# Which of two token blocks is chosen first: four heads of the scattered block move into the query stage, the gathered block moves to the gate stage

## The chip, the cores and the metric

The kernel runs on one core of one Trainium2 chip. The metric is the device time in microseconds, from the start of the program to its end, as the median of three runs. Below, PE is TensorE, DVE is VectorE, ACT is ScalarE, POOL is GpSimd and SP is SyncE, which here issues most of the transfers.

## What is computed

512 tokens of width 1024 pass through a mixer (two gated recurrences, a short convolution, an output projection), a layer norm, and then a layer of single-neuron experts with product keys. The change touches only the expert layer:

```python
def peer(x, w_q, k1, k2, u_tab, v_tab):          # 8 heads, 128 keys a side, 16 experts a head
    q = (xt @ w_q).reshape(t, PEER_HEADS, 2, PEER_HALF)
    s1 = jnp.einsum("thd,kd->thk", q[:, :, 0], k1)
    s2 = jnp.einsum("thd,kd->thk", q[:, :, 1], k2)
    v1, i1 = lax.top_k(s1, PEER_TOPK)
    v2, i2 = lax.top_k(s2, PEER_TOPK)
    cand_s = v1[..., :, None] + v2[..., None, :]
    top_s, pos = lax.top_k(cand_s, PEER_TOPK)
    idx = take(i1 * N_KEYS + i2, pos)
    g = jax.nn.softmax(top_s, axis=-1)
    ...
    act = jax.nn.gelu(jnp.einsum("cd,ced->ce", xb, u_tab[ib]))
    return jnp.einsum("ce,ced->cd", gb * act, v_tab[ib])
```

Each token takes 16 of 16,384 experts for each of 8 heads, 128 in all.

## The kernel before

The tokens are four blocks of 128, and the blocks go three ways. **Blocks 0 and 1** get a dense matrix of gates, made on PE from one-hot vectors of the chosen keys. **Block 2** (`ST`) gets its rows of the same gate matrix in DRAM, by scattering: each of its 128 slots (8 heads by 16) is one indirect transfer that adds 128 single numbers to the matrix, `GateCells.scatter`, L247. **Block 3** (`DT`, "far") doesn't use the dense product: for each of its 128 slots an indirect transfer gathers one expert row of 8 KB for each token (`GatherPath.start`, L1117, ring of three tiles), DVE takes the dot product (`dot`, L1136), ACT the gelu and the gate (`weigh`), and DVE adds the weighted second half of the row to a sum (`add`, L1157). `far.use(i)` is the i-th of these 256 operations of DVE: dot 0, dot 1, add 0, dot 2, add 1, and so on. For blocks 0 to 2 PE multiplies all 128 blocks of expert rows with the tokens (`ActPipeline.product`, L952, 24 matmuls for each), and later the gated activations with all second halves (L1746).

**Stages.** All five engines run programs written out by hand, one loop pass for each block m of expert rows. Products 0 to 15 lie in the *query stage* (query step n does 24 matmuls of the query projection, L1383, then product n, then 8 score matmuls, L1371), 16 to 18 follow it, and products 19 to 95 are the steps s = 0 to 76 of the *gate stage*, m = 19 + s. The *expert stage* has 128 steps; in the first 64 every second one also does a product, 96 to 127.

Product m needs the low parts of its weights, `ut_lo`. Until product 26 POOL makes them (`acts.lower`, L979); in step s = 7 (`BY_POOL`) DVE takes over (L986) and POOL keeps only the indirect transfers. Each engine works strictly in the order of its program, so what stands behind a waiting instruction waits too. POOL in query step n does `acts.lower(n - 1)`, then the low part of the query weights `wq_lower(n)` (L1320), then what else it has.

**Choosing.** After the top-16 searches, `Selection` turns positions into keys and gates for one block: places, match, weigh, add up for each side, then softmax. "Early" picks handle four heads after query step 7 (`PICK_AT`), and end in query step 9 with a list of addresses, on which the first indirect transfer waits. "Late" picks handle the rest in the gate stage, at the steps of `SELECT_AT` (eight parts for each block). `far_ops(m)` says how many of the 256 far operations DVE does beside block m; the gathers are started by what these sums allow. `scattered_by` spreads the 128 scatters over the gate stage; the first scatter of each head waits until all 16 of the head before it have landed. The one-hot groups (96, PE L1609, 8 matmuls for each pair of groups) run from s = 10 to 63.

## Time and profile before

| | us |
|---|---|
| Median of 3 runs (lowest, highest) | 1611.48 (1607.8, 1616.52) |
| The profiled execution's own time | 1613.08 |
| Its span from first to last instruction | 1611.1 |
| PE busy | 1519.5 |
| DVE busy | 1223.0 |
| ACT busy | 768.3 |
| POOL busy | 634.4 |

The span is 2 us shorter than the execution's time, which also holds the start and the end around it. Busy time is an average over stages with different limits, so it says where the work is and not what ends the kernel: the query stage lies at about 299 to 470 us, the gate stage at 483 to 929 us, the expert stage after that.

### The profile page before, as it was taken

To read this page: it belongs to the slowest core of one execution; us is meant where nothing else is said; L and a number is where in the kernel's file an instruction comes from. 1 tells how busy PE (TensorE), PEld (TensorE's weight loads), DVE (VectorE), ACT (ScalarE), POOL (GpSimd) and SP (SyncE) were. 2 spreads that over 40 slices of the span, in tenths; PEclk is the share of its full clock that TensorE was granted. 3 is DMA by queue.
4 is the path that set the end of the run, shared out by engine and by line. 5 is a ranking of instruction groups with operands and counts; after the bars stand their busy time and mean duration, and the time that the engine had idled before them with its cause. 6 is when DMAs were issued, how large, how long until landed. Compare 5 with 4: busy or idle time off the path is not lost.

```text
span 1611.1 us, 21027 instructions
## 1 busy us (share of the span) xinstructions
PE 1519.5 (94%) x7484; PEld 1329.3 (83%) x7484; DVE 1223.0 (76%) x2135; ACT 768.3 (48%) x1427; POOL 634.4 (39%) x400
## 2 busy tenths in 40 slices
PE   7999999999987899899988889999999999999996
PEld 5877657799987889898988878888888888888785
DVE  7569985678997768686664388888888877888775
ACT  3559970323224467676754244444444444444432
POOL 4843352664545777787778111111111111111100
PEclk9999999999999999999999899999999999999998
DMA  7438310433445678899999999999999989999972
GB/s 271 170 93 239 92 43 0 154 125 109 179 139 171 185 233 228 215 268 274 271 265 269 349 343 354 344 333 354 346 346 338 350 319 348 345 358 354 337 254 93
DMA packets 214791, 397.00 MB, mean 246 GB/s; under 512 B 97312, under 2 KB 155040, under 8 KB 198304
## 3 DMA queue, kind: packets, MB, share of 16 engines
q1 hardware_dynamic: 176384, 259.17, 48.6%
q0 software_dynamic: 36864, 134.30, 25.5%
q10 hardware_dynamic: 1440, 2.19, 0.4%
q8 instruction: 60, 0.98, 0.2%
q14 instruction: 43, 0.35, 0.1%
HBM read 349.40 MB, written 46.20 MB: 246 GB/s over the span
## 4 chain that ended last, share of the span: by engine, by line
PE 54%; POOL 17%; DVE 14%; DMA 6%; issue 6%; ACT 2%; SPq 0%; DVEq 0%; POOLq 0%; ACTq 0%
PE bank L1746 29%; POOL gate_matrix L247 13%; PE bank L952 13%; PE bank L787 5%; DMA gate_matrix<-gate_values,gate_cells 3%; PE bank L1383 2%; POOL gathered L1117 2%; PE bank L842 2%; DMA gate_rows_then_feed<-activations 2%; DVE xc L684 1%; DMA gathered<-in_peer_rows,expert_rows 1%; PE bank L828 1%; POOL rms L487 1%; PE bank L799 1%; DVE hit_late L1035 1%
## 5 line engine op out<-in xcount | busy, mean ns | idle before, releaser
L952 PE MATMUL bank<-xhi,ut_hi 128*128 128x384 f32 x1024 | 356.1, 348 | 30.4 <-DVE ut_lo L986 15.7
L1117 POOL DMA_INDIRECT gathered<-in_peer_rows,expert_rows x128 | 140.4, 1097 | 584.0 <-DVE gather_sum L1157 553.5
L952 PE MATMUL bank<-xhi,ut_lo 128*128 128x384 f32 x1024 | 349.3, 341 | 0.0
L952 PE MATMUL bank<-xlo,ut_hi 128*128 128x384 f32 x1024 | 349.0, 341 | 0.0
L247 POOL DMA_INDIRECT gate_matrix<-gate_values,gate_cells x128 | 244.6, 1911 | 63.9 <-issue 36.7
L1746 PE MATMUL bank<-v_hi,w_hi 128*128 128x512 f32 x760 | 236.3, 392 | 8.3 <-DVE w_lo L1851 8.3
L1786 ACT ACTIVATE v_hi<-gate_rows_then_feed 128x1024 fp32r<-128x1024 f32 x128 | 135.7, 1061 | 221.0 <-PE bank L1746 221.0
L1746 PE MATMUL bank<-v_lo,w_hi 128*128 128x512 f32 x760 | 235.3, 391 | 0.0
L1746 PE MATMUL bank<-v_hi,w_lo 128*128 128x512 f32 x760 | 235.2, 391 | 0.0
L952 PEld LDWEIGHTS bank<-xhi,ut_hi 128*128 128x128 f32 x1024 | 198.0, 193 | 36.1 <-DVE ut_lo L986 17.3
L1136 DVE SCALAR_TENSOR_TENSOR gathered<-gathered,h 128x1024 f32<-128x1024 f32 x128 | 156.1, 1220 | 70.9 <-DMA gathered<-in_peer_rows,expert_rows 70.8
L952 PEld LDWEIGHTS bank<-xlo,ut_hi 128*128 128x128 f32 x1024 | 197.7, 193 | 1.8
L952 PEld LDWEIGHTS bank<-xhi,ut_lo 128*128 128x128 f32 x1024 | 197.0, 192 | 0.0
L986 DVE TENSOR_TENSOR ut_lo<-u_raw,ut_hi 128x1024 fp32r<-128x1024 f32 x101 | 123.8, 1225 | 80.6 <-ACT ut_hi L962 74.2
L1834 DVE TENSOR_TENSOR v_lo<-gate_rows_then_feed,v_hi 128x1024 fp32r<-128x1024 f32 x128 | 156.4, 1222 | 33.4 <-ACT v_hi L1786 32.7
L967 ACT ACTIVATE gel<-bank 128x384 f32<-128x384 f32 x128 | 62.5, 488 | 243.9 <-PE bank L952 237.0
L1746 PEld LDWEIGHTS bank<-v_hi,w_hi 128*128 128x128 f32 x760 | 142.5, 189 | 37.7 <-DVE v_lo L1834 7.2
L1746 PEld LDWEIGHTS bank<-v_lo,w_hi 128*128 128x128 f32 x760 | 143.4, 189 | 30.6
L1746 PEld LDWEIGHTS bank<-v_hi,w_lo 128*128 128x128 f32 x760 | 143.2, 188 | 30.3
L1157 DVE SCALAR_TENSOR_TENSOR gather_sum<-gathered,expert_gelus,gather_sum 128x1024 f32<-128x1024 f32 x127 | 166.3, 1309 | 0.2
L962 ACT ACTIVATE ut_hi<-u_raw 128x1024 fp32r<-128x1024 f32 x128 | 135.0, 1055 | 16.7 <-DMA u_raw<-in_peer_u_turned 16.6
L979 POOL TENSOR_TENSOR ut_lo<-u_raw,ut_hi 128x1024 fp32r<-128x1024 f32 x27 | 66.2, 2454 | 86.7 <-ACT ut_hi L962 86.4
(246 smaller groups left out, 2406.5 us busy)
## 6 DMA issues: line engine op xcount, KB each, us to landing
u_raw<-in_peer_u_turned SPq DMA_DIRECT2D x128, 512.0 KB
gate_rows_then_feed<-in_peer_rows SPq DMA_DIRECT2D x128, 512.0 KB
gate_rows_then_feed<-gate_matrix SPq DMA_DIRECT2D x128, 192.0 KB
activations<-gel SPq DMA_DIRECT2D x96, 192.0 KB
gate_rows_then_feed<-activations SPq DMA_DIRECT2D x96, 192.0 KB
u_raw<-in_w_in_chunks SPq DMA_DIRECT2D x28, 512.0 KB, 4.1
gate_matrix<-gate_zeros SPq DMA_DIRECT2D x8, 1024.0 KB, 7.4
wq<-in_peer_wq_chunks SPq DMA_DIRECT2D x16, 512.0 KB, 3.9
```

Of the source, the lines that this page charges most:

```text
L247: self.nc.gpsimd.indirect_dma_start(out=self.flat, out_offset=bass.IndirectOffsetOnAxis(ap=self.at[:, k:k + 1], axis=0), in_=self.gate[:, ...
L787: ins = mm(z_bank(n)[:, :], w[n % 2][:, k, :], x[:, k, :], start=(i == 0), stop=(i == 3 * KD - 1))
L952: ins = self.nc.tensor.matmul(self.bank[b + r % 2][:, 0:DTOK], u[r % 2][:, k, :], x[:, k, 0:DTOK], start=(i == 0), stop=(i == 3 * KD - 1))
L962: self.nc.scalar.activation(self.hi[r % 2][:, :, :], self.by_channel(r), ACT.Copy).then_inc(self.hi_ready, 1)
L979: self.nc.gpsimd.tensor_tensor(out=self.lo[r % 2][:, :, :], in0=self.by_channel(r), in1=self.hi[r % 2][:, :, :].bitcast(F32), op=ALU.subtr ...
L986: self.nc.vector.tensor_tensor(out=self.lo[r % 2][:, :, :], in0=self.by_channel(r), in1=self.hi[r % 2][:, :, :].bitcast(F32), op=ALU.subtr ...
L1117: self.nc.gpsimd.indirect_dma_start(out=self.tile[q % RING][:, :], out_offset=None, in_=self.table, in_offset=bass.IndirectOffsetOnAxis(ap ...
L1136: self.nc.vector.scalar_tensor_tensor(out=half, in0=half, scalar=1.0, in1=self.x, op0=ALU.mult, op1=ALU.mult, accum_out=self.act[:, q:q + ...
L1157: ins = V.scalar_tensor_tensor(out=self.sum[:, :], in0=half, scalar=weight, in1=self.sum[:, :], op0=ALU.mult, op1=ALU.add)
L1746: ins = mm(bank[2 + 2 * tb + half][:, :], w[r][:, tb * P:(tb + 1) * P], v[r][:, half * HALF_D:(half + 1) * HALF_D], start=begins, stop=ends)
L1786: S.activation(v_hi[r][:, :], v_raw[r][:, :], ACT.Copy).then_inc(v_hi_ready, 1)
L1834: V.tensor_tensor(out=v_lo[r][:, :], in0=v_raw[r][:, :], in1=v_hi[r][:, :].bitcast(F32), op=ALU.subtract).then_inc(v_lo_ready, 1)
```

## The change

The four heads chosen in the query stage are now heads 0 to 3 of block 2, the scattered one, not of block 3. Their gates and their addresses (`list_cells`, one DVE instruction more than `list_rows`) go to `GateCells`, whose tiles are allocated earlier for it. POOL scatters two slots in each query step from n = 10 on, one with each of the blocks 16 to 25, and two with each block from 26 on; `SCATTERED_BY` replaces `scattered_by`. 22 of the 128 scatters so come before step s = 7, where none did, and the last one lies in s = 59, where it was s = 66. The wait of the gathers on their first list, and the asserted distance of three query steps between list and first gather, are gone from the query stage; a second list of block 2 (heads 4 to 7) comes in gate step 1, and a scatter of slot 64 waits for it.

Block 3 is now chosen whole, eight heads, in gate steps 2 to 5, and its first three gathers start in s = 6. The far operations of the query stage (10) are gone. In the gate stage there are one in every second step from s = 8, one in every step from s = 15, none in 28 to 35, and three in two steps after s = 65: 64 in all before the expert stage, where it was 75. In the expert stage DVE does two in each of the first 64 steps, as before, and after them seven in six steps, where it was one in each, so that block 3 is done at step 119 and not 117. Blocks 0 and 1 are chosen in steps 7 to 14 and 28 to 35 (before 4 to 8 and 20 to 27), and the one-hot groups run from s = 16 to 64, in 49 steps for 54.

```diff
@@ -64,25 +64,31 @@
 GROUPS = P // NT
 HALF_GROUPS = GROUPS // 2
 BY_POOL = 7
-SELECT_AT = {ST: (0, 0, 1, 1, 2, 2, 3, 3), 0: (4, 4, 5, 5, 6, 6, 7, 8), 1: tuple(range(20, 28)),
-             DT: tuple(range(32, 40))}
-TURN_AT = {9: 0, 29: 1}
-HOT_AT, HOT_STEPS = 10, 54
-SCATTER_AT, SCATTER_STEPS = 7, 60
+SELECT_AT = {ST: (0, 0, 0, 0, 1, 1, 1, 1), DT: (2, 2, 3, 3, 4, 4, 5, 5), 0: tuple(range(7, 15)),
+             1: tuple(range(28, 36))}
+TURN_AT = {15: 0, 36: 1}
+HOT_AT, HOT_STEPS = 16, 49
+FIRST_GATHER = 6
 
 
 def far_ops(m):
 
     s = m - BY_QUERIES
-    if m < QC - 3:
+    if s < FIRST_GATHER + 2 or 28 <= s < 36:
         return 0
-    if s < 0:
-        return 2 if m < QC else 4 if m == QC else 0
-    if s < HOT_AT or 20 <= s < 28:
+    if s < 15:
+        return 1 - s % 2
+    return 2 - s % 2 if s > 65 else 1
+
+
+def scatters(m):
+
+    if m < 10:
         return 0
-    return 2 if s in (11, 13, 15, 17, 19, 29) else 1
-
-
+    return 2 if m < QC else 1 if m < BY_QUERIES + BY_POOL else 2
+
+
+SCATTERED_BY = [min(SLOTS, sum(scatters(e) for e in range(m))) for m in range(MADE + 1)]
 FAR_BY = [sum(far_ops(e) for e in range(m)) for m in range(MADE + 1)]
 FAR_FROM = FAR_BY[MADE]
 
...
@@ -236,12 +242,25 @@
                       self.zeros[:, :].unsqueeze(1).broadcast_to([P, self.ROWS, P])).then_inc(self.zeroed, 16)
 
 
+    def list_cells(self, eng, link, sel, q, n):
+
+        V, at, size = self.nc.vector, slice(q * TOPK, (q + n) * TOPK), n * TOPK
+        link(V.scalar_tensor_tensor(out=self.row[:, at], in0=sel[:, 0, 0:size], scalar=float(KEYS),
+                                    in1=sel[:, 1, 0:size], op0=ALU.mult, op1=ALU.add))
+        if q == 0:
+            eng.wait_ge(self.token_ready, 1)
+        link(V.tensor_scalar(out=self.at[:, at], in0=self.row[:, at], scalar1=float(DTOK),
+                             scalar2=self.token[:, 0:1], op0=ALU.mult, op1=ALU.add))
+        V.sem_inc(self.listed, 1)
+
+
     def scatter(self, eng, k):
 
         q = k // TOPK
         if k == 0:
             eng.wait_ge(self.zeroed, 16 * self.ZEROED)
-            eng.wait_ge(self.listed, 1)
+        if k in (0, EARLY_HEADS * TOPK):
+            eng.wait_ge(self.listed, 1 + k // (EARLY_HEADS * TOPK))
         if k % TOPK == 0 and q > 0:
             eng.wait_ge(self.landed[(q - 1) % 2], 16 * TOPK * ((q - 1) // 2 + 1))
         self.nc.gpsimd.indirect_dma_start(
...
@@ -1337,13 +1346,13 @@
                 blk = h[:, n - 1, :]
                 link(G.tensor_tensor(out=blk, in0=blk, in1=ln[:, 0, :], op=ALU.mult))
                 link(G.tensor_tensor(out=blk, in0=blk, in1=ln[:, 1, :], op=ALU.add))
-            for q in range(started_by(n - 1), started_by(n)):
-                far.start(eng, q)
+            for k in range(SCATTERED_BY[n], SCATTERED_BY[n + 1]):
+                cells.scatter(eng, k)
         for m in range(QC - 1, BY_QUERIES + 1):
             acts.lower(eng, m, m)
-            if m == QC:
-                for q in range(started_by(QC - 1), started_by(QC)):
-                    far.start(eng, q)
+            if QC <= m < BY_QUERIES:
+                for k in range(SCATTERED_BY[m], SCATTERED_BY[m + 1]):
+                    cells.scatter(eng, k)
 
     def tensor(eng):
         mm, tr = nc.tensor.matmul, nc.tensor.transpose
@@ -1435,17 +1442,15 @@
                 link(top16(lambda tb: cand[:, tb, :], lambda tb: crep[:, tb, :],
                            lambda tb: top[:, tb, q, :], lambda tb: pos[:, tb, q, :]))
             if n == PICK_AT:
-                picks.places(link, DT, 0, EARLY_HEADS)
+                picks.places(link, ST, 0, EARLY_HEADS)
                 picks.match(link, 0, EARLY_HEADS)
                 picks.choose(link, 0, EARLY_HEADS)
             elif n == PICK_AT + 1:
                 picks.match(link, 1, EARLY_HEADS)
                 picks.choose(link, 1, EARLY_HEADS)
             elif n == PICK_AT + 2:
-                link(picks.softmax(eng, link, 1, EARLY_HEADS, far.gate[:, 0:EARLY_HEADS * TOPK]))
-                picks.list_rows(link, far, 0, EARLY_HEADS)
-        for e in range(FAR_BY[QC], FAR_BY[QC + 1]):
-            far.use(eng, e)
+                link(picks.softmax(eng, link, 1, EARLY_HEADS, cells.gate[:, 0:EARLY_HEADS * TOPK]))
+                cells.list_cells(eng, link, picks.sel, 0, EARLY_HEADS)
 
     def released(eng):
 
...
@@ -1495,7 +1500,7 @@
         hot_ready, hot_scaled, g_done, g_copied = (sem(n) for n in ("one_hot_ready", "one_hot_scaled", "g_done", "g_copied"))
         g_stored = [[sem(f"g_{part}_stored{i}") for part in ("low", "high")] for i in range(2)]
         nth = {tb: i for i, tb in enumerate(SELECT_AT)}
-        heads_of = lambda tb: (EARLY_HEADS, QH - EARLY_HEADS) if tb == DT else (0, QH)
+        heads_of = lambda tb: (EARLY_HEADS, QH - EARLY_HEADS) if tb == ST else (0, QH)
 
         def vector(eng):
             link = Chain(eng, chain)
@@ -1513,21 +1518,16 @@
                     picks.weigh(link, part // 4, n)
                 elif part in (3, 6):
                     if part == 3:
-                        after(eng, selT_done, {ST: 0, 0: 0, 1: 1, DT: 2}[tb])
+                        after(eng, selT_done, int(tb == 1))
                     picks.add_up(link, part // 4, n)
                 elif tb == DT:
-                    link(picks.softmax(eng, link, nth[DT] + 1, n, far.gate[:, q * TOPK:(q + n) * TOPK]))
-                    picks.list_rows(link, far, q, n)
-                elif tb < ST:
+                    link(picks.softmax(eng, link, nth[DT] + 1, n, far.gate[:, :]))
+                    picks.list_rows(link, far)
+                elif tb == ST:
+                    link(picks.softmax(eng, link, nth[tb] + 1, n, cells.gate[:, q * TOPK:(q + n) * TOPK]))
+                    cells.list_cells(eng, link, sel, q, n)
+                else:
                     picks.softmax(eng, link, nth[tb] + 1, QH, sel[:, 2, :]).then_inc(sel_ready, 1)
-                else:
-                    link(picks.softmax(eng, link, nth[tb] + 1, QH, cells.gate[:, :]))
-                    link(V.scalar_tensor_tensor(out=cells.row[:, :], in0=sel[:, 0, :], scalar=float(KEYS),
-                                                in1=sel[:, 1, :], op0=ALU.mult, op1=ALU.add))
-                    eng.wait_ge(cells.token_ready, 1)
-                    link(V.tensor_scalar(out=cells.at[:, :], in0=cells.row[:, :], scalar1=float(DTOK),
-                                         scalar2=cells.token[:, 0:1], op0=ALU.mult, op1=ALU.add))
-                    V.sem_inc(cells.listed, 1)
 
             def one_hots(n):
 
@@ -1560,9 +1560,9 @@
                 m = BY_QUERIES + s
                 if s < BY_POOL:
                     acts.lower(eng, m + 1, m + 1)
-                for q in range(far.started(FAR_BY[m - 1 if s else QC]), far.started(FAR_BY[m])):
+                for q in range(started_by(s - 1), started_by(s)):
                     far.start(eng, q)
-                for k in range(scattered_by(s), scattered_by(s + 1)):
+                for k in range(SCATTERED_BY[m], SCATTERED_BY[m + 1]):
                     cells.scatter(eng, k)
 
         def scalar(eng):
@@ -1672,7 +1672,7 @@
     LAST = (DT, *range(DT))
     is_live, block_of = feed.is_live, feed.block_of
 
-    far_by = lambda n: min(2 * SLOTS, FAR_FROM + 2 * min(n, TAIL) + max(n - TAIL, 0))
+    far_by = lambda n: min(2 * SLOTS, FAR_FROM + 2 * min(n, TAIL) + max(n - TAIL, 0) * 7 // 6)
     FAR_DONE = min(n for n in range(STEPS) if far_by(n) >= 2 * SLOTS)
     assert FAR_DONE + 5 <= CLOSE
```

POOL, query steps 9 to 12, from the low part of query weights 9 on (`ut_lo` with `ut_hi` is the low part of expert rows, `wq_lo` that of query weights; the number behind a name is the buffer). Before:

```order
L1320 TENSOR_TENSOR wq_lo1<-wq0,wq_hi1 128x1024 [waits wq_hi_ready]
L979 TENSOR_TENSOR ut_lo1<-u_raw0,ut_hi1 128x1024 [waits ut_hi_ready]
L1320 TENSOR_TENSOR wq_lo0<-wq1,wq_hi0 128x1024 [waits wq_hi_ready]
L979 TENSOR_TENSOR ut_lo0<-u_raw1,ut_hi0 128x1024 [waits ut_hi_ready]
L1320 TENSOR_TENSOR wq_lo1<-wq2,wq_hi1 128x1024 [waits wq_hi_ready]
L979 TENSOR_TENSOR ut_lo1<-u_raw2,ut_hi1 128x1024 [waits ut_hi_ready]
L1320 TENSOR_TENSOR wq_lo0<-wq0,wq_hi0 128x1024 [waits wq_hi_ready]
L1117 DMA gathered0<-in_peer_rows,expert_rows 128x2048 [waits rows_listed]
L1117 DMA gathered1<-in_peer_rows,expert_rows 128x2048
L1117 DMA gathered2<-in_peer_rows,expert_rows 128x2048
L979 TENSOR_TENSOR ut_lo0<-u_raw0,ut_hi0 128x1024 [waits ut_hi_ready]
```

Now, the same place:

```order
L1329 TENSOR_TENSOR wq_lo1<-wq0,wq_hi1 128x1024 [waits wq_hi_ready]
L998 TENSOR_TENSOR ut_lo1<-u_raw0,ut_hi1 128x1024 [waits ut_hi_ready]
L1329 TENSOR_TENSOR wq_lo0<-wq1,wq_hi0 128x1024 [waits wq_hi_ready]
L266 DMA gate_matrix<-gate_values,gate_cells 6291456x1 [waits cells_listed,gates_zeroed]
L266 DMA gate_matrix<-gate_values,gate_cells 6291456x1
L998 TENSOR_TENSOR ut_lo0<-u_raw1,ut_hi0 128x1024 [waits ut_hi_ready]
L1329 TENSOR_TENSOR wq_lo1<-wq2,wq_hi1 128x1024 [waits wq_hi_ready]
L266 DMA gate_matrix<-gate_values,gate_cells 6291456x1 x2
L998 TENSOR_TENSOR ut_lo1<-u_raw2,ut_hi1 128x1024 [waits ut_hi_ready]
L1329 TENSOR_TENSOR wq_lo0<-wq0,wq_hi0 128x1024 [waits wq_hi_ready]
```

The first indirect transfers stood behind the query weights of step 12; two scatters now stand behind those of step 10, ahead of the low part of expert rows 10 (the first `ut_lo0` after them), and two more in every step.

POOL, gate steps 3 to 11, where the low parts end and only transfers follow. Before:

```order
L979 TENSOR_TENSOR ut_lo1<-u_raw1,ut_hi1 128x1024 [waits ut_hi_ready]
L979 TENSOR_TENSOR ut_lo0<-u_raw2,ut_hi0 128x1024 [waits ut_hi_ready]
L247 DMA gate_matrix<-gate_values,gate_cells 6291456x1 [waits cells_listed,gates_zeroed]
L247 DMA gate_matrix<-gate_values,gate_cells 6291456x1 x7
L1117 DMA gathered1<-in_peer_rows,expert_rows 128x2048 [waits gather_added]
L247 DMA gate_matrix<-gate_values,gate_cells 6291456x1 x2
L1117 DMA gathered2<-in_peer_rows,expert_rows 128x2048 [waits gather_added]
L247 DMA gate_matrix<-gate_values,gate_cells 6291456x1 x4
L1117 DMA gathered0<-in_peer_rows,expert_rows 128x2048 [waits gather_added]
L247 DMA gate_matrix<-gate_values,gate_cells 6291456x1 x2
L247 DMA gate_matrix<-gate_values,gate_cells 6291456x1 [waits gates_landed0]
L1117 DMA gathered1<-in_peer_rows,expert_rows 128x2048 [waits gather_added]
```

Now:

```order
L998 TENSOR_TENSOR ut_lo1<-u_raw1,ut_hi1 128x1024 [waits ut_hi_ready]
L266 DMA gate_matrix<-gate_values,gate_cells 6291456x1
L998 TENSOR_TENSOR ut_lo0<-u_raw2,ut_hi0 128x1024 [waits ut_hi_ready]
L1135 DMA gathered0<-in_peer_rows,expert_rows 128x2048 [waits rows_listed]
L1135 DMA gathered1<-in_peer_rows,expert_rows 128x2048
L1135 DMA gathered2<-in_peer_rows,expert_rows 128x2048
L266 DMA gate_matrix<-gate_values,gate_cells 6291456x1 x11
L266 DMA gate_matrix<-gate_values,gate_cells 6291456x1 [waits gates_landed1]
L266 DMA gate_matrix<-gate_values,gate_cells 6291456x1
L1135 DMA gathered0<-in_peer_rows,expert_rows 128x2048 [waits gather_added]
L266 DMA gate_matrix<-gate_values,gate_cells 6291456x1 x6
L1135 DMA gathered1<-in_peer_rows,expert_rows 128x2048 [waits gather_added]
```

A scatter stands between every two low parts, the first three gathers come after the last low part, and fewer gathers lie between the scatters than before.

DVE, the end of the query stage and the first instructions of the gate stage (the MAX_INDEX rows are the last search; `iotab_late` and `ex_late` open the choosing of block 2). Before:

```order
L1415 MAX_INDEX pos<-top,crep 128x8 [waits dve_chain_queries]
L1415 MAX_INDEX pos<-top,crep 128x8 x3
L1157 SCALAR_TENSOR_TENSOR gather_sum<-gathered2,expert_gelus,gather_sum 128x1024 [waits gather_added,gather_weighed,dve_chain_queries]
L1136 SCALAR_TENSOR_TENSOR gathered1,expert_acts<-gathered1,h 128x1024 [waits tile_gathered1]
L1157 SCALAR_TENSOR_TENSOR gather_sum<-gathered0,expert_gelus,gather_sum 128x1024 [waits gather_added,gather_weighed]
L1136 SCALAR_TENSOR_TENSOR gathered2,expert_acts<-gathered2,h 128x1024 [waits tile_gathered2]
L1009 CAST iotab_late<-iota 128x16 [waits wq_lo_ready,qT_ready,pool_chain_queries,scores_done,q_done]
L1015 TENSOR_TENSOR ex_late<-top 128x128 [waits dve_chain_gates]
```

Now:

```order
L1424 MAX_INDEX pos<-top,crep 128x8 [waits dve_chain_queries]
L1424 MAX_INDEX pos<-top,crep 128x8 x3
L1028 CAST iotab_late<-iota 128x16 [waits qT_ready,wq_lo_ready,scores_done,pool_chain_queries,q_done,dve_chain_queries]
L1034 TENSOR_TENSOR ex_late<-top 128x64 [waits dve_chain_gates]
L1039 TENSOR_SCALAR place_late<-pos 128x64
L1040 TENSOR_SCALAR place_late<-pos 128x64
```

The last far operations of the query stage, which wait for gathered tiles, are gone, and the choosing of block 2, now four heads (128x64), follows the last search at once.

## Rows read from the trace of the kernel before

**Rows 1.** The page's part 4, the chain that ended last, by engine.

```profile
PE 54%; POOL 17%; DVE 14%; DMA 6%; issue 6%; ACT 2%; SPq 0%; DVEq 0%; POOLq 0%; ACTq 0%
```

**Rows 2.** Windows: from:to, length, busy of PE, PEld, DVE, ACT, POOL, clock, DMA share, GB/s.

```profile
458.12:482.88 24.76, 20.33 (x105) 20.01 (x105) 21.10 (x105) 6.62 (x12) 15.31 (x7) 0.86 0.58 194
482.88:524.50 41.62, 32.42 (x170) 30.95 (x169) 32.81 (x36) 17.53 (x26) 21.11 (x9) 0.92 0.51 172
524.50:865.40 340.90, 315.11 (x1934) 311.28 (x1935) 240.67 (x245) 217.41 (x561) 265.46 (x147) 0.96 0.90 241
865.40:928.80 63.40, 52.52 (x267) 51.55 (x266) 27.45 (x29) 18.35 (x34) 22.32 (x14) 0.89 1.07 337
```

**Rows 3.** Chain of 545 to 870 us, by line, and the longest of its pieces.

```profile
by line: POOL gate_matrix L247 63.1%; issue 13.1%; DMA gate_matrix<-gate_values,gate_cells 12.6%; POOL gathered L1117 10.7%; DVE ut_lo L986 0.4%; DVE gather_sum L1157 0.4%
...
616.29 7.88 DMA gate_matrix<-gate_values,gate_cells
```

**Rows 4.** POOL's timeline, query steps 9 to 12: start, duration, instruction, idle before and releaser.

```profile
389.15 2.39 POOL L1320 TENSOR_TENSOR wq_lo<-wq,wq_hi 128x1024 fp32r<-128x1024 f32 x1
397.37 2.39 POOL L979 TENSOR_TENSOR ut_lo<-u_raw,ut_hi 128x1024 fp32r<-128x1024 f32 x1 [5.83 <-ACT ut_hi L962]
...
419.47 1.20 POOL L1117 DMA_INDIRECT gathered<-in_peer_rows,expert_rows  x1 [6.79 <-DVEq L1069]
```

**Rows 5.** DVE's timeline: a stretched step, and the end of the early list.

```profile
410.49 2.48 DVE L1431 TENSOR_TENSOR cand<-best 128x256 f32<-128x256 f32 x1
...
418.88 0.23 DVE L1066 SCALAR_TENSOR_TENSOR expert_rows<-sel_early 128x64 int32<-128x64 f32 x1
```

**Rows 6.** PE's timeline, first matmuls of products 15, 16, 22, 27, and the last one before product 10.

```profile
404.94 0.39 PE L1383 MATMUL bank<-xhi,wq_lo 128*128 128x512 f32 x1
...
462.56 0.69 PE L952 MATMUL bank<-xhi,ut_hi 128*128 128x384 f32 x1 [4.43 <-POOL ut_lo L979]
...
470.03 0.42 PE L952 MATMUL bank<-xhi,ut_hi 128*128 128x384 f32 x1
...
504.08 0.69 PE L952 MATMUL bank<-xhi,ut_hi 128*128 128x384 f32 x1 [6.96 <-POOL ut_lo L979]
...
532.74 0.69 PE L952 MATMUL bank<-xhi,ut_hi 128*128 128x384 f32 x1 [3.82 <-DVE ut_lo L986]
```

**Rows 7.** Chain of 305 to 316 us: one product and one set of scores at full clock.

```profile
310.29 4.18 PE bank L952 x24
314.47 0.89 PE bank L1371 x8
```

**Rows 8.** Groups of POOL, 524.5 to 885.5 us: count, busy, mean ns, idle before, by releaser.

```profile
L247 POOL DMA_INDIRECT gate_matrix<-gate_values,gate_cells x128 | 244.6, 1911 | 63.9 <-issue 36.7 <-DMA gate_matrix<-gate_values,gate_cells 27.2
L1117 POOL DMA_INDIRECT gathered<-in_peer_rows,expert_rows x28 | 38.6, 1380 | 14.3 <-issue 8.2 <-DVE gather_sum L1157 6.1
```

**Rows 9.** POOL's timeline: first scatter, a short one, and the last one before 884.65 us.

```profile
524.60 2.40 POOL L247 DMA_INDIRECT gate_matrix<-gate_values,gate_cells  x1 [0.17 <-issue]
...
614.43 1.55 POOL L247 DMA_INDIRECT gate_matrix<-gate_values,gate_cells  x1 [0.30 <-issue]
...
882.23 2.42 POOL L247 DMA_INDIRECT gate_matrix<-gate_values,gate_cells  x1 [0.30 <-issue]
```

**Rows 10.** PE's timeline: products 30, 31 and 86 begin.

```profile
548.00 0.42 PE L952 MATMUL bank<-xhi,ut_hi 128*128 128x384 f32 x1
...
553.06 0.42 PE L952 MATMUL bank<-xhi,ut_hi 128*128 128x384 f32 x1
...
873.22 0.45 PE L952 MATMUL bank<-xhi,ut_hi 128*128 128x384 f32 x1 [3.47 <-DVE ut_lo L986]
```

**Rows 11.** Waits of DVE for gathered tiles, 524.5 to 865.4 us: total, times, longest.

```profile
DVE gathered L1136 <- DMA gathered<-in_peer_rows,expert_rows: 41.1, 12, 9.8
```

**Rows 12.** Windows, columns as in Rows 2: the end of the gate stage, the later expert stage.

```profile
911.00:932.00 21.00, 17.39 (x91) 17.39 (x92) 10.98 (x12) 8.53 (x14) 1.87 (x2) 0.92 1.03 396
1350.00:1500.00 150.00, 150.00 (x663) 124.21 (x662) 122.48 (x166) 62.30 (x110) 18.63 (x19) 1.00 0.99 352
```

35 lines of the change are left out of this document (12 added, 23 removed).

## The prediction, made before the changed kernel ran

> **What bounds the kernel now.** I read the chain of waits first, because it names who ends last. By engine it is PE for 54% and POOL for 17% [rows 1], though POOL is busy for only 634 of 1611 us. The windows by stage then show where PE is not full [rows 2]: it is idle for 4.4 us at the end of the query stage (20.33 busy of 24.76), for 9.2 us in the early gate stage (458 to 524 us are products 15 to 25), for 25.8 us between 524.5 and 865.4 us, and for 10.9 us in the last part. The chain of 545 to 870 us alone settles what these are: scatters 63.1%, the gaps between POOL's instructions ("issue") 13.1%, waits for a scatter to land 12.6%, gathers 10.7% [rows 3]. All of that is POOL's program. So from 524 to 866 us POOL is the bound: it issues gathers late behind scatters, DVE waits for the tiles (12 times, 41.1 us [rows 11]), the low part that DVE owes PE comes late, and PE stops. After a stop PE also runs at half clock for a while: product 15 and its scores took 470.03 - 462.56 = 7.47 us [rows 6], for 4.18 + 0.89 = 5.07 at full clock [rows 7], so a stop costs its length plus up to 2.4 us.
>
> **Term 1, the query stage: +14 us.** POOL waited in query step 12 for the list of the early picks, until 419.47; the wait showed as 6.79 us and hurt nobody [rows 4]. Now the same wait stands in step 10. POOL gets there at 389.15 + 2.39 = 391.5 us [rows 4]. The list doesn't move with it: DVE ended it at 418.88 + 0.23 = 419.1 us [rows 5], in an unbroken run of searches. I take 2 us off, since the step at 410.49 took 2.48 us while POOL worked on query weights [rows 5], and POOL will be waiting then, and add 0.3 for the additional instruction of `list_cells`: 417.4. Behind the waiting scatter stand a second one and the low part of block 10, and PE needs that low part for product 10 when it has done the query matmuls, at 404.94 + 0.39 = 405.3 [rows 6]. Two scatters take 2 x (1.91 + 0.30) = 4.4 us [rows 8, 9], the low part 2.4 [rows 4]: it is ready at 424.2. PE stands for 18.9 us, and pays 2.4 us of clock: 21.3. Once past that, POOL has 2 x 2.4 + 4.4 = 9.2 us of work in each query step and PE 5.49 + 4.18 + 0.89 = 10.6, so the scatters of steps 11 to 15 hide. In return the stop of 4.43 us before product 15, where POOL waited for a far sum, goes with the far operations, and its 2.4 us of clock [rows 6]: -6.8. Net +14.5, taken as +14. Bounds: +11 if a scatter there takes 1.55 us, the shortest shown [rows 9], and the list comes 2 us earlier still; +18 if the list isn't earlier and a scatter takes 2.4.
>
> **Term 2, products 16 to 25: -5 us.** The stop of 6.96 us before product 22 [rows 6] followed DVE's wait for the last gathered tile of the query stage, with which the choosing of block 2 began late. No tile is waited for there now. But between every two low parts POOL now has a scatter: 2.4 + 1.91 + 0.30 = 4.6 us for each product of 4.18. Before, product 16 began at 470.03 [rows 6] and product 26 at 524.5 [rows 2], 54.5 us. Now: one product at 4.2, nine at 4.6, 1 us for the one landing that scatter 16 waits for, and, as an estimate, 1.1 us twice for ACT's exponents of blocks 2 and 3: 48.8. That is -5.7, taken as -5. Bounds: -12 with PE alone as the limit (10 x 4.2), 0 if the same stops come back in other places.
>
> **Term 3, products 26 to 84: -26 us.** This is POOL's account. Before: 128 scatters, 244.6 us, with 0.30 us between [rows 8], so 2.21 each. Of the seven head changes each cost 27.2 / 7 = 3.9 us [rows 8]. A gather costs 1.38 + 0.30 = 1.68. The first scatter began at 524.60 and the last ended at 882.23 + 2.42 = 884.65 [rows 9], 19.2 us after product 85, its own step, had begun at 865.4 [rows 2]. Now 22 scatters are done earlier, so 106 remain: 106 x 2.21 = 234.3, and 19 gathers x 1.68 = 31.9, and six head changes x 3.9 = 23.4: 289.6 us. They begin about 6 us after product 26, behind three gathers (3 x 1.3) and scatter 21, and end in s = 59 with two scatters where the last step had three, so about 17 us behind PE: PE begins s = 59 at 6 + 289.6 - 17 = 278.6 us after product 26. Seven steps remain to s = 66, with 12 one-hot groups: 7 x 4.18 + 12 x 0.45 = 34.7, where 0.45 is half of what a step with two groups takes over a product (553.06 - 548.00 = 5.06 [rows 10], less 4.18). With 2 us for a stop in between that is 315 us, for 340.9 before [rows 2]. Of the removed stops the ones before products 27 and 86 are shown, 3.82 and 3.47 us [rows 6, 10]. What is late next is POOL again: in s = 16 to 59 it has 2 x 2.21 + 0.5 x 1.68 + 0.5 = 5.8 us for each step of 5.06. Bounds: -48 if scatters take 1.55 us, since then PE's own 59 x 4.18 + 96 x 0.45 = 290 us is nearly the limit; -3 below, under the rivals.
>
> **Term 4, products 85 to 95: -3 us.** The stops here were POOL's at first (13 scatters lay in its last seven steps) and those go, but three far operations in two steps want 8 gathers in 11 steps for 5.5 before, in a stretch whose transfers were at a share of 1.07 [rows 2]. I let the two nearly cancel; bounds -10 and +6.
>
> **Term 5, the expert stage: +5 us.** 11 far operations more fall here, all after step 64, since the rate before that is the same. On DVE that is 1.3 us in every sixth step, beside 122 of 150 busy [rows 12], and hides. The transfers are another matter: half a gather in each step of 4.1 us becomes 0.58, 0.083 MB more on 1.44, so 352 GB/s at a share of 0.99 [rows 12] would have to be 373. In the last 21 us of the gate stage the same engines moved 396 [rows 12], so 373 can be had, but with fewer long pauses for the loads. I take +5; bounds 0 and +15.
>
> **Sum.** 14 - 5 - 26 - 3 + 5 = -15. Against the profiled execution's 1613.08 that is 1598; it lies 1.6 us above the median of the three runs, so for the median 1611.5 - 15 = 1597 us.
>
> **Rivals.** *POOL stops binding.* If scatters run near their shortest, term 3 becomes about -48 and the total 1575. For: nothing in a scatter but its 128 numbers needs more, and many took 1.55 us. Against: the mean over 128 was 1.91, and the choosing of block 0 now lies under scatters of steps 7 to 14. *The transfers bind in the later expert stage.* If 352 GB/s at 0.99 is all there is, 55 steps of 4.1 us grow by 6%, +13.5 for +5: 1605. For: the share; against: the 396. The Trainium skill ("DMA: Bandwidth & Descriptors", section "Where 436 GB/s comes from") puts the limit of transfers from device memory at about 358 GB/s for a core; by that the demand is 4% too high and the stage grows by an estimated 9 us, which would give 1601. The trace's 396 GB/s for 21 us speaks against it as a strict limit. *Slower: the gathers' landing binds the gate stage, not POOL's issue.* If the tiles come late because transfers take 7 to 9 us to land however early they are issued, the earlier scatters buy only their own share of the transfers, about -3 for term 3, and the stop in the query stage stays: 14 - 5 - 3 - 3 + 5 = +8, or 1620. It decides where a gather that is issued at its planned step still ends a wait of DVE. For: the share was 0.90 over these 341 us [rows 2] and a landing took up to 7.9 us even for small scatters [rows 3]. Against: the chain runs through POOL's instructions for 87% and through no gather's landing [rows 3]. *The change doesn't do what it says*, in that no scatter runs in the query stage, can't be: the order is fixed, and POOL waits until it can.
>
> **How the numbers follow.** Forecast 0.50, POOL not binding 0.12, transfers in the expert stage 0.20, slower 0.18. A measurement of this kernel can tell about 0.5% from no change, so faster means below 1603.4 and slower above 1619.5. Faster: 0.45 of the forecast's 0.50, 0.12, and 0.03 of the third: 0.60. Slower: 0.12 of the last case's 0.18. The rest is 0.28. The range leaves out the fastest of the second case and the slowest of the last: 1580 to 1617.
>
> **What would show it.** Right: in the profile after, a stop of PE of about 19 us before product 10, ended by POOL's low part, with POOL waiting for DVE's list just before; none before products 15 and 22; the chain from some 545 to 830 us still on scatters; product 85 begun some 315 us after product 26. Wrong: a mean scatter far from 1.91 us; PE full in the gate stage; DVE waiting for tiles whose gathers were issued on time; more than a few us of PE idle after step 64 of the expert stage.

## The result, and the profile after the change

The changed kernel takes 1655.36 us (median, 1647.47 to 1657.16); the kernel before, on the same chip, 1611.34 (1607.8 to 1616.52). The ratio is 1.0275, its 95% interval 1.0223 to 1.0326: slower by 2.7%, where I had forecast 1597 us. The profiled execution has a span of 1654.1 us against 1611.1.

The time by stage, from the first matmul of product 16, 26 and 85 and from DVE's `w_lo` (L1851) of expert steps 0, 64 and 119, each in its own trace:

| stretch | before | after | forecast | measured |
|---|---|---|---|---|
| start to product 16 | 470.0 | 484.4 | +14 | +14.4 |
| products 16 to 25 | 54.5 | 50.1 | -5 | -4.4 |
| products 26 to 84 | 340.9 | 316.7 | -26 | -24.2 |
| products 85 to 95 | 63.4 | 68.3 | -3 | +4.9 |
| expert steps 0 to 63 | 399.1 | 442.2 | 0 | +43.1 |
| expert steps 64 to 118 | 226.3 | 235.4 | +5 | +9.1 |

What lies in no row is the same in both: 4.6 us between product 95 and the first `w_lo`, and 52 us at the end.

So the gate stage ends 9.3 us earlier, as the account of POOL wanted, and the expert stage takes 52 us more, for which I had 5.

The chain of waits, part 4 of the page after the change, by engine and by line. It answers to [rows 1]:

```profile
PE 30%; DMA 22%; DVE 17%; POOL 14%; issue 10%; ACT 5%; SPq 2%; DVEq 0%; ACTq 0%; POOLq 0%
DMA gathered<-in_peer_rows,expert_rows 14%; POOL gate_matrix L266 11%; PE bank L1746 8%; PE bank L971 7%; PE bank L806 5%; DMA gate_rows_then_feed<-activations 5%; PE bank L1392 4%; DVE gather_sum L1175 3%; PE bank L861 2%; ACT ut_hi L981 2%; DVE w L1846 2%; DMA u_raw<-in_peer_u_turned 2%; DMA gate_matrix<-gate_values,gate_cells 1%; POOL gathered L1135 1%; SPq L960 1%
```

PE falls from 54% of the chain to 30%, and the landing of gathered tiles, in no large part of the chain before, is the first line. Windows of the kernel after (columns as in [rows 2]): the last products, expert steps 0 to 63, steps 64 to 118.

```profile
851.20:919.50 68.30, 52.37 (x266) 50.45 (x265) 32.46 (x36) 19.35 (x38) 8.25 (x8) 0.90 1.02 339
924.00:1367.00 443.00, 404.20 (x1893) 345.93 (x1894) 327.02 (x419) 166.36 (x320) 83.13 (x65) 0.98 0.86 307
1367.00:1602.00 235.00, 228.66 (x990) 185.64 (x989) 192.20 (x259) 96.97 (x172) 30.34 (x29) 0.99 0.97 356
```

The same two expert stretches of the kernel before:

```profile
933.00:1333.00 400.00, 394.37 (x1893) 347.16 (x1893) 326.69 (x421) 172.51 (x322) 63.81 (x64) 0.99 0.93 341
1333.00:1559.00 226.00, 224.67 (x990) 185.31 (x989) 181.20 (x244) 93.00 (x160) 23.39 (x24) 1.00 0.96 339
```

In steps 0 to 63 the work is the same, 1893 matmuls and 327 us of DVE. The transfers have a lower share (0.86 for 0.93) and a lower rate (307 GB/s for 341): they are less loaded, and still the stage is longer. So they are waited for one by one, not for their sum. The waits of these windows say by whom. First two rows after the change, then two of before (engine, line, waited for: us, times, longest):

```profile
DVE gathered L1154 <- DMA gathered<-in_peer_rows,expert_rows: 99.8, 34, 6.9
PE bank L1746 <- DVE w_lo L1851: 39.0, 33, 9.3
```

```profile
PE bank L1746 <- DVE w_lo L1851: 5.6, 2, 4.7
DVE gathered L1136 <- DMA gathered<-in_peer_rows,expert_rows: 3.9, 2, 3.6
```

DVE waits for a gathered tile about every second step, 2.9 us each time, and PE then waits for DVE. DVE's account gives the step: (327.0 + 99.8 of waits for tiles + 15.9 of waits for ACT) / 64 = 6.9 us, and the step took 442.2 / 64 = 6.9. Before, PE set it: from step 8 to 64 a step took 6.19 us, while DVE had 326.7 / 64 = 5.1 us of work in it. So DVE had 1.1 us of slack a step, and a mean wait of 1.6 us took more than that.

Why the tiles are late is seen in two steps of DVE's timeline after the change (start, length, operation, idle before):

```profile
1101.63 1.28 DVE L1175 SCALAR_TENSOR_TENSOR gather_sum<-gathered,expert_gelus,gather_sum 128x1024 f32<-128x1024 f32 x1
1102.83 1.22 DVE L1154 SCALAR_TENSOR_TENSOR gathered<-gathered,h 128x1024 f32<-128x1024 f32 x1
...
1106.05 1.28 DVE L1175 SCALAR_TENSOR_TENSOR gather_sum<-gathered,expert_gelus,gather_sum 128x1024 f32<-128x1024 f32 x1
1110.43 1.23 DVE L1154 SCALAR_TENSOR_TENSOR gathered<-gathered,h 128x1024 f32<-128x1024 f32 x1 [3.10 <-DMA gathered<-in_peer_rows,expert_rows]
```

POOL's timeline beside them, the gather that the addition at 1101.63 set free:

```profile
1103.18 1.68 POOL L1135 DMA_INDIRECT gathered<-in_peer_rows,expert_rows  x1 [10.08 <-DVE gather_sum L1175]
```

And the kernel before, DVE and POOL:

```profile
1106.90 1.28 DVE L1157 SCALAR_TENSOR_TENSOR gather_sum<-gathered,expert_gelus,gather_sum 128x1024 f32<-128x1024 f32 x1
...
1111.76 1.22 DVE L1136 SCALAR_TENSOR_TENSOR gathered<-gathered,h 128x1024 f32<-128x1024 f32 x1
...
1112.90 1.28 DVE L1157 SCALAR_TENSOR_TENSOR gather_sum<-gathered,expert_gelus,gather_sum 128x1024 f32<-128x1024 f32 x1
...
1118.15 1.22 DVE L1136 SCALAR_TENSOR_TENSOR gathered<-gathered,h 128x1024 f32<-128x1024 f32 x1
```

```profile
1108.45 1.01 POOL L1117 DMA_INDIRECT gathered<-in_peer_rows,expert_rows  x1 [5.09 <-DVE gather_sum L1157]
1114.45 0.94 POOL L1117 DMA_INDIRECT gathered<-in_peer_rows,expert_rows  x1 [4.99 <-DVE gather_sum L1157]
```

Product q is operation 2q - 1 of the far block and addition q is operation 2q + 2, and with a ring of three tiles gather q + 3 starts when addition q is done; its product is three operations behind that addition. The kernel before has done 75 operations when the expert stage begins, an odd number, so each step does a product and then an addition: the addition at 1106.90 ends the second half of its step, and three operations later is the first one of the step after next, at 1118.15, 10.0 us after the addition's end at 1108.18. The changed kernel has done 64, an even number. Each step now does an addition and then a product, and three operations later is the *second* one of the *next* step. DVE has only the product, `w`, `v_lo`, `w_lo` and the next addition in between, 4.4 us from 1102.91 to 1107.33, plus a `ut_lo` where there is one, and then it stands until the tile has landed, 7.2 us after POOL began to issue it at 1103.18. The number 64 is the sum of the gate stage's new table, and 75 of the old. Below, *distance* is this time from the end of the addition that frees a tile to the product that reads the tile's next filling.

The gathers also took longer in the changed kernel, 7.5 us on the mean from POOL's start to the landing for 6.5 before. As an estimate, 1.0 us at each of the 34 waits is 34 of the 99.8 us, so the shorter distance alone is not all of the wait. Why they took longer is open (see the last section).

### The profile page after: what moved, and what is told of

Its sections match the earlier page's. It is cut to its first block, busy times and chain, and to the rows that moved or that the text cites. A ratio compares the mean times of both kernels' runs of the same rounds, so it can differ in the third digit from the quotient of the medians.

```text
span 1654.1 us, 21033 instructions
## 1 busy us (share of the span) xinstructions
PE 1525.9 (92%) x7484; PEld 1319.2 (80%) x7484; DVE 1221.2 (74%) x2136; ACT 764.7 (46%) x1427; POOL 654.2 (40%) x400
## 4 chain that ended last, share of the span: by engine, by line
PE 30%; DMA 22%; DVE 17%; POOL 14%; issue 10%; ACT 5%; SPq 2%; DVEq 0%; ACTq 0%; POOLq 0%
DMA gathered<-in_peer_rows,expert_rows 14%; POOL gate_matrix L266 11%; PE bank L1746 8%; PE bank L971 7%; PE bank L806 5%; DMA gate_rows_then_feed<-activations 5%; PE bank L1392 4%; DVE gather_sum L1175 3%; PE bank L861 2%; ACT ut_hi L981 2%; DVE w L1846 2%; DMA u_raw<-in_peer_u_turned 2%; DMA gate_matrix<-gate_values,gate_cells 1%; POOL gathered L1135 1%; SPq L960 1%
## 5 line engine op out<-in xcount | busy, mean ns | idle before, releaser
L1135 POOL DMA_INDIRECT gathered<-in_peer_rows,expert_rows x128 | 159.2, 1244 | 636.1 <-DVE gather_sum L1175 628.1
L1746 PE MATMUL bank<-v_hi,w_hi 128*128 128x512 f32 x760 | 240.5, 398 | 46.7 <-DVE w_lo L1851 46.3
L1790 ACT ACTIVATE w_hi<-w 128x384 fp32r<-128x384 f32 x128 | 66.8, 522 | 277.3 <-DVE w L1846 276.7
L1175 DVE SCALAR_TENSOR_TENSOR gather_sum<-gathered,expert_gelus,gather_sum 128x1024 f32<-128x1024 f32 x127 | 162.5, 1279 | 0.0
```

What stands on the lines that cost most here:

```text
L1135: self.nc.gpsimd.indirect_dma_start(out=self.tile[q % RING][:, :], out_offset=None, in_=self.table, in_offset=bass.IndirectOffsetOnAxis(ap ...
L1175: ins = V.scalar_tensor_tensor(out=self.sum[:, :], in0=half, scalar=weight, in1=self.sum[:, :], op0=ALU.mult, op1=ALU.add)
L1746: ins = mm(bank[2 + 2 * tb + half][:, :], w[r][:, tb * P:(tb + 1) * P], v[r][:, half * HALF_D:(half + 1) * HALF_D], start=begins, stop=ends)
L1790: S.activation(w_hi[n % SLOT][:, :], w32[:, n % 2, :], ACT.Copy).then_inc(w_hi_ready, 1)
```

## The experiments

A theory and its rivals. **Distance**: the time from the addition that frees a tile to the product that reads the tile's next filling has become shorter than a gather takes; that explains steps 0 to 63. **Traffic**: the gathers of the later expert stage are denser (seven operations in six steps), or block 3 as a whole starts later, and the transfers can't follow. **Order as such**: the addition in front waits for something of ACT's. The waits above speak against that already: in steps 0 to 63 DVE waited 15.9 us for ACT in the changed kernel and 67.8 us in the kernel before, 56.0 of them for a gelu:

```profile
DVE w L1846 <- ACT gel L967: 56.0, 29, 3.5
```

For the gate stage the question is whether the stop in the query stage was a necessary price.

The texts below count the kernels in the order in which they were put down: the first is the changed kernel with the order swapped back, the second the kernel before with the order swapped, the third the kernel before with the denser gathers, the fourth the first with later scatters, the fifth the changed kernel with the product late; the sixth and seventh are the fourth with far operations moved within the gate stage, and the eighth is the kernel before with the addition late.

### The order swapped back, by one operation

```
-far_by = lambda n: min(2 * SLOTS, FAR_FROM + 2 * min(n, TAIL) + ...
+far_by = lambda n: min(2 * SLOTS, FAR_FROM + min(n, 1) + 2 * min(n, TAIL) + ...
```

In the changed kernel:

> The changed kernel with one far operation more in expert step 0 (three there, two in each step after it), so that each of the steps 1 to 63 does a product and then an addition, in the order of the kernel before; the gate stage is untouched. Distance theory: in the changed kernel the addition comes first in a step and the product second, so that a gather, which starts after the addition, has one step until its product; it needs 7 to 8 us and DVE waited 96.4 us for gathers (3.9 us in the kernel before). With the order swapped back this wait falls below 10 us, the 64 steps take about 400 us and not 442, and the kernel takes 1608 to 1616 us. Rival (the traffic of the gathers, one per step whatever the order, is what slows the stage): 1650 to 1657 us, the wait for gathers stays over 80 us.

Measured: 1610.68 us, ratio to before 1.0019 (0.9992 to 1.0046). Of the 44 us all are gone. Products 26 to 84 took 318.8 us (316.7 in the changed kernel), steps 0 to 63 404.7. DVE's products in steps 0 to 63 (count, busy and mean ns, idle before):

```profile
L1154 DVE SCALAR_TENSOR_TENSOR gathered<-gathered,h 128x1024 f32<-128x1024 f32 x65 | 79.2, 1219 | 6.3 <-DMA gathered<-in_peer_rows,expert_rows 6.2
```

The traffic is the same to the byte, so the rival of traffic falls for this stretch. The same line in the kernel before:

> The kernel before with the same one line: one far operation more in expert step 0, so that the steps 1 to 63 do the addition first and the product second. Distance theory: the fault of the changed kernel appears in the kernel before without any of its other edits; DVE waits for gathers 85 to 100 us in the 64 steps, and the time goes up by 35 to 45 us, to about 1650 us. Rival (traffic, or the later start of block 3): 1609 to 1614 us, no change.

Measured: 1653.67 us, ratio 1.0282 (1.0246 to 1.0318): the whole loss of the change appears in the kernel before by shifting one operation. Steps 0 to 63 took 441.4 us, steps 64 to 118 226.7.

```profile
L1136 DVE SCALAR_TENSOR_TENSOR gathered<-gathered,h 128x1024 f32<-128x1024 f32 x65 | 79.5, 1223 | 99.2 <-DMA gathered<-in_peer_rows,expert_rows 99.2
```

### The denser gathers alone

The kernel before, with the factor `* 7 // 6` of the change:

> The kernel before with the last factor of the change alone: seven far operations in six steps from expert step 64 on, where it does one in each. Distance theory: this has no part in the 43 us lost in steps 0 to 63, and of the 9 us lost in steps 64 to 96 at most that; 1609 to 1620 us. Rival (the denser gathers saturate the transfers, which run at 350 to 358 GB/s there): 1620 to 1640 us.

Measured: 1611.67 us, ratio 1.0015 (0.9988 to 1.0041), no difference that can be told. Steps 64 to 118 took 228.4 us for 226.3. My term for this, +5, was too large rather than too small. The first experiment's kernel, with the same rate, shows what the transfers do in that stretch:

```profile
1325.00:1554.00 229.00, 226.98 (x990) 184.51 (x989) 190.37 (x257) 96.40 (x170) 30.63 (x29) 1.00 0.98 358
```

PE is busy for 227 of 229 us, so 358 GB/s at a share of 0.98 still keeps up with it.

### Distance or order

Two kernels keep their counts of operations and which of the two comes first in a step, and move one of them within the step, which changes the distance. In the changed kernel the product moves to the end of the step, behind `w_lo`:

```
-        def gathered(n):
+        def gathered(n, late=False):
             for i in range(far_by(n), far_by(n + 1)):
-                far.use(eng, i)
+                if late == (0 < n < TAIL and i % 2 == 1):
+                    far.use(eng, i)
...
             w_lower(n)
+            gathered(n, late=True)
```

> The changed kernel with its order of far operations kept (addition before product, 64 done before the expert stage), but in the expert steps 1 to 63 the product stands at the end of DVE's step, behind w, v_lo and w_lo, and not at its head behind the addition. Distance theory: it isn't the order as such that costs, but the time from the addition that frees a tile to the product that reads its next filling; the product's place gives 2.3 us of work more (1.22 for v_lo, 0.55 each for w and w_lo) over the 1.6 us that DVE waited for each gather on average (96.4 us / 60), so the wait falls below 20 us and the kernel takes 1612 to 1622 us. Rival (the order matters in another way, such as the addition's wait for ACT's weight of the product): over 1640 us.

Measured: 1628.97 us (1616.61 to 1641.46), ratio 1.0167 (1.0096 to 1.0238). That is 7 us over my range, and 26 us below the changed kernel. It is also the kernel whose executions differ most: 1616.61 and 1620.07 lie in my range, 1637.86 and 1641.46 far above it, and without the longest the median would be 1620.07. In the profiled one, a quick one of 1616.61, steps 0 to 63 took 411.0 us:

```profile
L1154 DVE SCALAR_TENSOR_TENSOR gathered<-gathered,h 128x1024 f32<-128x1024 f32 x64 | 78.2, 1221 | 25.9 <-DMA gathered<-in_peer_rows,expert_rows 25.9
```

Most of the wait is gone though 64 operations are done when the stage begins and the addition comes first in the step, as in the changed kernel. With the distance near what a gather takes, each late landing still costs; that this is what spreads the executions is a reading, not shown. In the kernel before, the other way about, the addition moves behind `w_lo` (the same edit with `i % 2 == 0`):

> The kernel before with its order of far operations kept (product before addition) and its numbers, but in the expert steps 1 to 63 the addition stands at the end of DVE's step, behind w, v_lo and w_lo. Distance theory: order and parity as such cost nothing, the distance alone does. From this addition to the product that reads the next filling of its tile DVE has 5.4 us of work (product 1.22, w 0.55, v_lo 1.22, w_lo 0.55, addition 1.28, half a ut_lo 0.61), as in the changed kernel, for gathers that need 6 to 8 us, so the wait for gathers grows from 3.9 us to 80 to 110 us and the kernel takes 1640 to 1660 us. Rival (it is the order addition, product that costs): 1606 to 1614 us.

Measured: 1636.51 us (1633.89 to 1650.16), ratio 1.0193 (1.0129 to 1.0256), a little below my range. The product comes first in the step and 75 operations are done at the start, both as before, and the wait is there:

```profile
L1136 DVE SCALAR_TENSOR_TENSOR gathered<-gathered,h 128x1024 f32<-128x1024 f32 x64 | 78.3, 1223 | 97.8 <-DMA gathered<-in_peer_rows,expert_rows 97.7
```

So neither the number 64 nor which operation stands first in a step makes the wait. Means of the profiled executions, in us; the distances are over the additions of steps 3 to 59, the gathers and the sum of waits over steps 0 to 63:

| kernel | DVE's work within the distance | distance, less the wait | a gather | waits for tiles |
|---|---|---|---|---|
| before | 7.7 | 9.9 | 6.5 | 3.9 |
| first | 7.7 | 10.0 | 6.6 | 6.2 |
| fifth | 7.1 | 8.6 | 7.2 | 25.9 |
| eighth | 5.6 | 7.2 | 8.0 | 100.4 |
| second | 5.0 | 6.9 | 7.5 | 99.2 |
| changed | 5.0 | 6.9 | 7.5 | 99.8 |

Where the distance is longer than a gather by some us, next to nothing is waited for; where it is shorter, nearly 100 us are. One thing the two kernels don't separate. Seen along DVE's whole program, a late addition stands right in front of the next step's product, as in the changed kernel, and a late product right in front of the next addition, as before. The eighth kernel and then the fifth:

```profile
1113.94 1.28 DVE L1157 SCALAR_TENSOR_TENSOR gather_sum<-gathered,expert_gelus,gather_sum 128x1024 f32<-128x1024 f32 x1
1119.05 1.22 DVE L1136 SCALAR_TENSOR_TENSOR gathered<-gathered,h 128x1024 f32<-128x1024 f32 x1 [3.83 <-DMA gathered<-in_peer_rows,expert_rows]
```

```profile
1102.57 1.22 DVE L1154 SCALAR_TENSOR_TENSOR gathered<-gathered,h 128x1024 f32<-128x1024 f32 x1
1103.71 1.28 DVE L1175 SCALAR_TENSOR_TENSOR gather_sum<-gathered,expert_gelus,gather_sum 128x1024 f32<-128x1024 f32 x1
```

So the neighbours of each operation change together with the distance. That it is the distance is told by what ends the waits, the landing of a gather each time. A fourth tile in the ring, which would lengthen the distance and leave the order, was not tried. What the late addition costs is less than what the swap costs (steps 0 to 63: 424.5 us for 441.4) with nearly the same wait for tiles, because DVE's other waits are gone here: 0.4 us for ACT in all, where the second experiment's kernel has 14.8 us of them, 11.3 for the `ut_hi` that comes right before each `ut_lo`.

### The stop in the query stage

The changed kernel stops PE before product 10, as forecast: POOL waits for the list with the low part behind it. POOL's timeline, and PE's first matmul of product 10:

```profile
390.24 2.40 POOL L1329 TENSOR_TENSOR wq_lo<-wq,wq_hi 128x1024 fp32r<-128x1024 f32 x1
418.81 1.80 POOL L266 DMA_INDIRECT gate_matrix<-gate_values,gate_cells  x1 [26.18 <-DVEq L254]
420.91 1.58 POOL L266 DMA_INDIRECT gate_matrix<-gate_values,gate_cells  x1 [0.30 <-issue]
421.93 2.93 POOL L998 TENSOR_TENSOR ut_lo<-u_raw,ut_hi 128x1024 fp32r<-128x1024 f32 x1
```

```profile
424.91 0.69 PE L971 MATMUL bank<-xhi,ut_hi 128*128 128x384 f32 x1 [18.51 <-POOL ut_lo L998]
```

The edit, with the order swapped back as in the first experiment:

```
 def scatters(m):
-    if m < 10:
+    if m < 12:
         return 0
```

> The changed kernel with the order swapped back as in the first of these runs, and its scatters beginning at query step 12 and not 10 (18 before the gate stage's step 7, not 22; the last one in step 62). My account of the query stage (POOL stands at the list of addresses, which comes at 423 us, with the last work on the block behind it, so that TensorE stops 18.5 us before product 10): the stop falls back to about 4.4 us and the kernel is 10 to 15 us below the first of these runs, at about 1598 us. Rival (the stop is needed by the DVE's longer list and merely moves to a later product, or is given back because the scatters pace the gate stage): within 4 us of the first run.

Measured: 1594.97 us, ratio to before 0.9906 (0.9877 to 0.9935), the first kernel that beats the one before, by 0.9%. POOL now makes the low part of block 10 at 396 us and waits afterwards, in query step 12:

```profile
408.61 2.41 POOL L1329 TENSOR_TENSOR wq_lo<-wq,wq_hi 128x1024 fp32r<-128x1024 f32 x1
418.68 1.79 POOL L266 DMA_INDIRECT gate_matrix<-gate_values,gate_cells  x1 [7.66 <-DVEq L254]
```

PE has no wait at all from 380 to 470 us; product 16 begins at 461.6 us, 8.4 us before the kernel before. Products 26 to 84 pay some of it back, 323.6 us for 318.8; POOL has four scatters more there.

The same edit in the changed kernel, its far operations as they are:

> The changed kernel with its scatters beginning at query step 12 and not 10, and nothing else; the order of its far operations is as changed. If the two losses are independent, as the stages say, it takes 12 to 18 us less than the changed kernel, 1637 to 1643 us, since a step of the expert stage waits for the gather that its own addition released and can give nothing back. Rival (one loss hides the other, because transfers bound the later stages): within 5 us of 1655 us.

Measured: 1636.0 us, ratio 1.017 (1.0129 to 1.021), 19 us below the changed kernel, a little more than forecast: the two losses add. Steps 0 to 63 took 436.6 us, with 96.8 us of waits for tiles.

### The last products, and the head of the expert stage

> The fourth kernel (order swapped back by a third operation in expert step 0, scatters from query step 12) with the six additional far operations of the steps s > 65 moved to s = 17, 19, 21, 23, 25 and 27; 64 in all as before. Traffic theory for the end of the gate stage: from s = 66 the transfers are full (share 1.05, 346 GB/s) and 12 products with their gathers lay there for 8 in the kernel before, each gather moving 1 MB, 3 us at that rate; with three gathers fewer there the products 85 to 95 and the last step come some 6 to 9 us sooner, and the kernel takes 1585 to 1592 us. Rival (DVE's work, not the transfers, is late there; or POOL, which has 4 us of scatters in a step of 5.1 us, falls behind from s = 17 on and the gain is lost there): 1593 to 1600 us.

Its edit, on the fourth kernel:

```
-    return 2 - s % 2 if s > 65 else 1
+    return 2 if s in (17, 19, 21, 23, 25, 27) else 1
```

Measured: 1594.13 us, ratio 0.9924 (0.99 to 0.9948), as the fourth kernel: the rival's time. The windows of the last products, of the fourth kernel and of this one, point to the local part of the theory, though:

```profile
834.00:901.00 67.00, 51.35 (x268) 49.44 (x267) 32.84 (x36) 19.34 (x38) 8.24 (x8) 0.92 1.05 347
```

```profile
839.00:899.00 60.00, 50.52 (x265) 48.60 (x264) 25.01 (x27) 17.97 (x32) 5.62 (x6) 0.94 1.03 325
```

Up to the expert stage it is 6.7 us less (64.7 for 71.4, from product 85 to the first `w_lo`), with two gathers fewer on POOL; but products 26 to 84 take 327.0 for 323.6, and product 16 happened to begin 1.5 us later. That the gain was handed back where the operations went is a reading of one execution of each. Over all profiles this stretch took 64.7 to 68.2 us in the three without the denser operations after s = 65 (the sixth, the seventh twice) and 68.9 to 73.6 us in the seven with them, so some 5 us is what they cost there. The seventh kernel adds a seventh operation at s = 15 and drops the third one of expert step 0:

> As the sixth, with a seventh operation at s = 15, so that 65 are done before the expert stage, the product comes first there of itself, and expert step 0 has two operations and not three. In the fourth kernel DVE's third operation of step 0 waited 8.7 us for a gather started only after the second, and TensorE stood 10.3 us at 910.8 us; in the kernel before, whose step 0 has two, it stood 4.7 us. Theory: the stop falls to about 5 us and the kernel is 4 to 7 us below the sixth, 1580 to 1588 us. Rival (the weights of the first steps are late anyway): within 2 us of the sixth.

Measured: 1595.55 us, ratio 0.9926 (0.9897 to 0.9956): above my range, within 2 us of the sixth, as the rival had it. Yet the stop at the head fell as forecast, PE in the fourth kernel and in this one:

```profile
921.16 1.19 PE L1746 MATMUL bank<-v_hi,w_hi 128*128 128x512 f32 x2 [10.31 <-DVE w_lo L1851]
```

```profile
913.63 1.19 PE L1746 MATMUL bank<-v_hi,w_hi 128*128 128x512 f32 x2 [4.68 <-DVE w_lo L1851]
```

(My text called the wait behind it that of the third operation; by DVE's timeline it is the product of step 1, for the gather that the first addition of step 0 started.) Steps 0 to 63 took 397.7 us for 404.1, but steps 64 to 118 took 237.7 for 230.8. Whether that is a law or an accident the next two were to tell. The fourth kernel without its third operation, by one more operation at s = 16:

```
-    return 2 - s % 2 if s > 65 else 1
+    return 2 - s % 2 if s > 65 or s == 16 else 1
```

> The changed kernel with two edits: one far operation more in the gate stage, at s = 16 (65 before the expert stage, so that product comes before addition there and expert step 0 keeps two operations), and scatters from query step 12. It is the fourth kernel without its third operation in step 0. If that third operation's 10.3 us stop of TensorE is a loss of its own, 5 us come off the fourth kernel's 1595: 1588 to 1592 us. If, as the seventh kernel suggests, what is won at the head of the expert stage is given back from step 64 on, 1593 to 1597 us, with over 234 us in steps 64 to 119 where the fourth has 230.8.

Measured: 1592.34 us (1590.11 to 1600.99), ratio 0.9917 (0.9886 to 0.9947). Steps 0 to 63 took 397.9 us, steps 64 to 118 229.2: nothing was given back in the expert stage. The median lies just above the first of my two ranges, 2.6 us below the fourth kernel's; the intervals overlap, so the four kernels with product first and scatters from step 12 (1592 to 1596 us) can't be ranked.

> The seventh kernel once more: its steps 64 to 119 took 237.7 us, those of the sixth 230.9 us, though both have the same 193 far operations done by step 64. If this is of the kernel, it is again over 235 us; if it differs from execution to execution, 228 to 235 us and a span of 1584 to 1590 us.

Measured in one execution: 1600.26 us, span 1598.3; steps 64 to 118 took 231.9 us, not 237.7, so that difference was one execution's. The span is above the range that I gave for this case, because products 26 to 84 took 337.9 us where the same kernel had 324.9 before. POOL's scatters of that stretch differ in their mean between the two executions, this one first:

```profile
L266 POOL DMA_INDIRECT gate_matrix<-gate_values,gate_cells x111 | 221.9, 1999 | 53.7 <-issue 32.0 <-DMA gate_matrix<-gate_values,gate_cells 21.8
```

```profile
L266 POOL DMA_INDIRECT gate_matrix<-gate_values,gate_cells x111 | 214.9, 1936 | 55.2 <-issue 32.0 <-DMA gate_matrix<-gate_values,gate_cells 23.2
```

That is 7 us more of POOL's work, beside 13 us more for the stage; that the one made the other is a reading. One profile of one stage is thus good to some 13 us at worst there, and no difference of a few us between single profiles above should be read as more than a hint.

> The changed kernel once more, for the part of its loss that the order doesn't explain: its steps 64 to 119 took 235.4 us in one profiled execution, 226.3 us before the change. If that is of the kernel, it is again 233 to 238 us; if it differs from execution to execution, it is anywhere from 226 to 238. DVE's wait for gathers in steps 0 to 63 is again 90 to 110 us either way.

Measured in one execution: 1659.72 us; 105.5 us of waits for tiles and 447.1 us in steps 0 to 63, and 237.8 us in steps 64 to 118. The latter is of the kernel, then: the changed kernel took 235.4 and 237.8, its copy with the later scatters 236.3, while those with 7/6 and the product first took 228.4 to 231.9 (once 237.7), and the one with the addition first but without 7/6, the second experiment, 226.7. The two together don't explain it either. From step 64 on the fifth kernel has the very program of the changed one, with 7/6 and the same operations in each step, and took 229.5. What differs is how steps 0 to 63 went. In the three long ones the first eight of these steps took 37.3 to 37.7 us (33.4 in the kernel before, 34.6 in the fifth, 35.3 in the second), so about 4 us of the loss lie right behind the stage in which DVE was late. That they are its after-effect was not tested, and the rest is open.

## Why the prediction was wrong

**Term 1, +14, right.** Measured +14.4, with the stop at 18.51 us for 18.9 and the low part ready at 424.9 for 424.2. What I didn't ask was whether the stop was needed: two query steps later the same wait costs nothing.

**Term 2, -5, and term 3, -26, right.** Measured -4.4 and -24.2. POOL's account held in its sum: products 26 to 84 took 316.7 us for my 315, and the chain from 545 to 850 us still runs through scatters for 57.7%. But a part of the working was wrong, and the match owes something to luck. I counted 96 one-hot groups at 0.45 us. Both traces have 512 records of their matmuls, 8 for each of 64 groups (`ALL_GROUPS`, so "96" in the description of the kernel is wrong too), and a group takes 0.90: a step without one lasts 4.16 us at best, with one 5.06, with two 5.96.

```profile
L1609 PE MATMUL bank<-hot x512: 270/275/377, 579.0 to 846.9; 128*128 128x128 f32 x171
```

So PE alone needs 59 x 4.16 + 64 x 0.90 = 303 us here and not 290, and my bound of -48 could not have come: -38 is all there was. Of the 44 steps s = 16 to 59, which I had paced by POOL, 35 ran at PE's own pace. All that stops and slow steps still add to the 303 us is 14 us, where it was 38 before. The rival that the gathers' landing would bind the gate stage, which would have left term 3 at -3, was wrong.

**Term 4, -3, wrong in sign.** Measured +4.9, inside its bounds of -10 to +6. PE waited 15.9 us there for low parts from DVE. The denser operations after s = 65 cost some 5 us locally, as the sixth and seventh kernels show; that the scatters that went away saved less than I let them is inferred. Measured up to the first `w_lo`, the term is +5.0 in the changed kernel, +2.5 in its second execution and +1.5 in the first experiment's kernel with the same gate stage, so a part of it is of one execution.

**Term 5, +5, the step that failed.** I wrote that eleven operations more fall to the expert stage, "all after step 64, since the rate before that is the same", and priced steps 0 to 63 at nothing. The rate is the same; the phase isn't. I counted operations by step and never wrote out which of them stand in one step, so the number 64 for 75 passed as a count. The price of the phase was 43.1 us, more than eight times the whole term. What I did price, the denser gathers, came out at +2 us in steps 64 to 118 when it was alone. The rule I weighed there, the limit of about 358 GB/s (the Trainium skill, "DMA: Bandwidth & Descriptors", section "Where 436 GB/s comes from"), bore neither way on the result: that stretch moved 358 GB/s in the first experiment's kernel and 363 in the fifth's, and took 229.4 and 229.5 us; the traces don't show a limit at 358.

The rivals failed with it. "Slower" was given 0.12, for another mechanism in another stage. One of my signs of being wrong did come, DVE waiting for tiles whose gathers were issued on time, but in the expert stage, where no term of mine had it. The trace of before held what was needed: a gather's landing could be read there (5.6 to 6.2 us after its issue around 1105 us, against 10.0 us from addition to product), and with it the question how much of these 10 us the new table leaves. With the phase of before restored, and nothing else, the changed kernel takes 1610.7 us, still 14 above the forecast. Its profiled execution has a span 4.5 us shorter than before, where the sum was -15; of the 10.5 us between, 3.8 are in term 3 (318.8 us for 315), 4.5 in term 4 (+1.5 for -3) and 3.7 in term 5, with +5.6 in steps 0 to 63, whose step 0 has a third operation there, and +3.1 in steps 64 to 118; terms 1 and 2 gave 1.7 back.

## What to carry to other kernels

A ring of buffers has a distance: the work between the operation that frees a slot and the one that reads its next filling. When a table of counts changes, write out for one steady step which operations stand in it and how far apart these two are, and compare that with the transfer's time from release to landing; a count that is off by one can shorten the distance by a third (here from 9.9 to 6.9 us) while operations and bytes stay the same. In the profile the sign is a consumer that waits for the same kind of transfer again and again (here in every second step) while the transfers' share has gone *down*; and where a wait is moved within an engine's program, look at what is queued behind it, since two steps later it may be free.

## What the runs showed of the hardware

A gather of 1 MB (128 rows of 8 KB) took 6.5 us on the mean from POOL's start of it to its landing in steps 0 to 63 of the kernel before and 7.9 us or more for one in ten, and 7.5 and 8.5 us in the changed kernel, though the transfers were at a lower share there (0.86 for 0.93). I had not expected it to be slower with less load. The changed kernel starts two gathers within 4.4 us and then none for 9 (1103.18, 1107.60 and 1116.79), the kernel before one in every 6. That does not explain it: the eighth kernel starts them 5.4 to 10 us apart, with one exception, and its gathers took 8.0 us on the mean, the longest of all. Why is open. For one transfer of 1 MB on the same path the Trainium skill ("DMA: Bandwidth & Descriptors", section "Anatomy of one DMA — SWDGE (gpsimd) path") gives 2.0 us plus the bytes at 436 GB/s, an estimated 4.4 us. These gathers ran beside other queues with 307 to 341 GB/s in all, and took 1.5 to 1.7 times that in these two kernels. The measurement decides; by that fit alone, the 4.4 to 5.6 us of DVE's work in the changed kernel would have looked about enough.
